# Native sparse attention: GpSimd scales head 1's probabilities, VectorE head 0's; turned tiles and compressed scores laid out anew

## Chip, cores and metric

One core of a Trainium2 chip. The metric is the device time of one execution in microseconds (us); lower is better. The kernel before takes 1884.68 us, the median of 3 runs (1881.19 to 1887.92).

## What is computed

One step of a small decoder trunk: an RWKV-7 layer, a mixture of experts (MoE), shared keys and values, one layer of native sparse attention, a second MoE, and a final norm, all in float32. There are 512 prompt tokens and 32 sample tokens, 16 attention heads of width 64 in 4 key groups, and 16 experts. The part around the change is the attention of the prompt. The selected branch may pick 16 blocks of 64 keys and there are only 8, so the selected and the window branch are both plain causal attention over their own keys; the third branch is over 31 compressed keys:

```python
s_c = einsum('bqgpd,bngd->bqgpn', qg, kc) - slope * d_c
p_c = masked_softmax(s_c, d_c >= 0)             # 31 compressed keys
s_s = einsum('bqgpd,bqgkd->bqgpk', qg, k_s) - slope * d_s
p_s = masked_softmax(s_s, d_s >= 0)
s_w = einsum('bqgpd,bwgd->bqgpw', qg, kw) - slope * d_w
p_w = masked_softmax(s_w, m_w)
o = g[..., 0:1] * (p_c @ v_c) + g[..., 1:2] * (p_s @ v_s) + g[..., 2:3] * (p_w @ v_w)
```

The softmax is divided by its row sum and multiplied by the gate g. In the MoE each token goes through 2 of 16 experts: `combine * ((silu(h @ w_gate) * (h @ w_up)) @ w_down)`.

## The kernel before, in words

Each engine runs a program written out by hand, in order, and engines meet only at semaphores (`wait_ge`, `then_inc`).

**Attention** (`pe_attend` L2948, `act_kv` L3093, `dve_attend` L3269). The 16 heads are taken as 8 pairs j. A unit u is (pair j, query tile i of 128 rows, branch br), 8 units for a pair and 64 in all (NU), then 4 units for the sample. A unit has two heads h of 128*(i+1) keys. For a unit, TensorE makes scores (L2960) into banks 0 to 3; VectorE adds the distances, finds the row minimum and writes to SBUF (L3319); ScalarE takes the exponential in place and the row sums (L3167); VectorE takes the reciprocal of the two sums (L3340), multiplies it by the gates (L3342), and scales both heads' probabilities (L3346, once for each h); TensorE turns them in pieces of 64 rows (L3015) into banks 4 and 5; ScalarE copies these to SBUF (L3157); TensorE multiplies by the values (L3051) into bank 7, which ScalarE stores once for a pair (L3187).

The steps are staggered, and this fixes the order on each engine. At step s VectorE does the scores of unit s and then the weights of unit s-2. ScalarE copies the turned unit s-4 and then does the exponentials of unit s-1. TensorE does, for even s: scores(s), turn(s-4), values(s-6), values(s-5), turn(s-3), scores(s+1). `p_ready` tells TensorE that a unit's probabilities are scaled; four score buffers (NSC) and three turned ones (NPT) limit how far engines run apart.

For the first unit of a pair there is also the compressed branch for all four query tiles: `cmp_scores` (L2981) into bank 6, five VectorE operations of 248 columns (L3327, L3330, L3332, L3352, L3360) with three small ones, two exponentials (L3173), `cmp_turn` (L2990, 8 matmuls against the identity), one copy of 512 columns (L3160), and two matmuls for each query tile with `vcp` (L3047).

GpSimd does nothing in this stage: its queue goes from the MoE of layer 0 (`pool_moe`) to that of layer 1.

**MoE** (`pe_moe` L1960, `act_moe` L2184, `dve_moe` L2323). 16 slots of 96 tokens in each layer, so 32 in all; a slot is one expert's gate, up and down matmuls, with 3 buffers of weights. In a slot TensorE does up, then turns the tokens of a later slot (L2012, 6 transposes of 128x128), waits for VectorE's product silu(gate) times up (L2449), turns that (L2062, 3 transposes), does gate of the next slot, and then down, which waits for the turned product to be copied out by ScalarE (L2236) and VectorE (L2455). The turned tokens are copied out by VectorE (L2440, one operation) and ScalarE (L2220, four).

Of the kernel before, what the change touches and what calls it, by code (L numbers as in the profile page):

```python
# [242 lines left out]
def program(nc, io, out):  # L243
    ctx = ExitStack()
    with ctx:
# [6 lines left out]
        def _(pool):  # L252
# [46 lines left out]
            pool_moe(pool, B, 0, regs)  # L299
            pool_moe(pool, B, 1, regs)  # L300
# [80 lines left out]
        def _(pe):  # L381
# [33 lines left out]
            def key_squares(m):  # L415
                pe.wait_ge(S("ksq_ready"), m + 1)
# [6 lines left out]
            for k in range(KT):  # L423
                pe.wait_ge(S("xm_first"), k + 1)
# [13 lines left out]
            pe.transpose(bank[3][0:72, 0:128], B.lasth[:].rearrange("p n k -> p (n k)"), ident[:]).then_inc(S("last_tr"), 1)  # L438
# [38 lines left out]
        def _(act):  # L477
# [24 lines left out]
            for g in range(2 * KT):  # L502
# [3 lines left out]
                if m >= 0:  # L506
                    if m >= 2:
                        act.wait_ge(S("ksum_mm"), m - 1)
                    act.drain()
                    act.activation((B.hwa, B.hg)[m % 2][:], B.rkv[1][:, m, :], ACT.Square, scale=vec(B, "k_k")[:, m:m + 1]).then_inc(S("ksq_ready"), 1)  # L510
# [20 lines left out]
        def _(dve):  # L531
# [70 lines left out]
            for k in range(KT + 1):  # L602
# [3 lines left out]
                if k:  # L606
                    dve.scalar_tensor_tensor(out=B.xm[0][:, k - 1, :], in0=B.xx[:, k - 1, :], scalar=vec(B, "mix0")[:, k - 1:k],
                                             in1=h[:, k - 1, :], op0=ALU.mult, op1=ALU.add).then_inc(S("xm_first"), 1)
# [13 lines left out]
            dve.wait_ge(S("last_tr"), 1)  # L622
# [1337 lines left out]
def pe_moe(pe, B, l, regs):  # L1960
# [88 lines left out]
    def slot(v, j, left):  # L2049
# [13 lines left out]
        mm.then_inc(S("at_mm"), 1)  # L2063
# [120 lines left out]
def act_moe(act, B, l, regs):  # L2184
# [42 lines left out]
    def slot(v, j, left):  # L2227
# [7 lines left out]
        act.wait_ge(S("at_mm"), s + 1)  # L2235
        act.activation(B.actT[:, 0:2].rearrange("p c t -> p (c t)"), bank[2][:, 0:256], ACT.Copy).then_inc(S("at_ev"), 1)  # L2236
# [86 lines left out]
def dve_moe(dve, B, l, regs):  # L2323
# [1150 lines left out]
```

## Time and profile before

| what | us |
|---|---|
| median of 3 runs | 1884.68 |
| the profiled execution, its own time | 1893.58 |
| its span, first to last instruction | 1891.8 |
| attention stage, 1296 to 1462 of the span | 166 |
| MoE slots of layer 0 and layer 1 | 734 to 1012, 1577 to 1855 |
| TensorE busy in the span | 1767.2 (93%) |
| VectorE, ScalarE, GpSimd busy | 672.5, 512.4, 99.9 |

Times in rows are us from the start of the span; a mean or a duration marked ns is of one instruction. PE is TensorE's matmuls, PEld its weight loads, DVE VectorE, ACT ScalarE, POOL GpSimd. Records of the same kind that follow each other are merged ("x16"). A group has its count, its busy us in sum, the mean ns of one, and the engine's idle us just before. TensorE's matmuls overlap in the records, so its busy time is not a measure of how full it is; the spacing of weight loads is a better one. "[0.63 <-PE bank L2960]" says that the engine stood idle 0.63 us before this instruction and that the matmul of L2960 released it.

### The profile page before, as it was taken

How to read it: one execution, taken by the hardware profiler on the slowest of the kernel's cores; microseconds unless marked ns; L12 is line 12 of the kernel's file. 1: busy time of each engine (PE TensorE's matmuls, PEld its weight loads, DVE VectorE, ACT ScalarE, POOL GpSimd, SP SyncE). 2: the span in 40 equal slices, each digit the busy share in tenths (PEclk: the TensorE clock that was granted, in tenths of full speed). 3: DMA queues.
4: the chain of work that ended last, by engine and by line, in shares of the span. 5: the costliest groups of instructions: out<-in, count | busy, mean ns of one | idle time of the engine just before them, and what ended most of it. 6: DMA issues, size and time to landing. Idle time of an engine off the chain costs nothing.

```text
span 1891.8 us, 53674 instructions
## 1 busy us (share of the span) xinstructions
PE 1767.2 (93%) x23759; PEld 1428.1 (75%) x23759; DVE 672.5 (36%) x1807; ACT 512.4 (27%) x1216; POOL 99.9 (5%) x155
## 2 busy tenths in 40 slices
PE   6999999989998899999999899898989989999997
PEld 4876777777776678999988754687766778999985
DVE  6141226776764332110104300406887240111014
ACT  3112223333332121111113200315887121111113
POOL 2112000000000002000002000000000011000002
PEclk8999999999999999999999999898999997999998
DMA  8666844443434497999978991633000476999944
GB/s 310 212 219 208 266 123 155 135 129 113 118 111 138 139 319 298 376 414 419 417 290 229 244 203 57 196 87 102 2 2 2 124 330 236 411 412 416 417 197 169
DMA packets 195434, 413.68 MB, mean 219 GB/s; under 512 B 53702, under 2 KB 135330, under 8 KB 186722
## 3 DMA queue, kind: packets, MB, share of 16 engines
q1 hardware_dynamic: 176434, 358.08, 55.2%
q0 software_dynamic: 11040, 39.85, 5.8%
q10 hardware_dynamic: 7760, 12.79, 1.9%
q8 instruction: 161, 2.64, 0.6%
q14 instruction: 39, 0.32, 0.1%
HBM read 356.97 MB, written 57.91 MB: 219 GB/s over the span
## 4 chain that ended last, share of the span: by engine, by line
PE 44%; issue 7%; DVE 6%; DMA 2%; DVEq 2%; ACT 1%; POOL 0%; ACTq 0%; SPq 0%
PE bank L2024 12%; PE bank L2019 6%; PE bank L2037 5%; PE bank L2043 4%; PE bank L1746 3%; PE bank L2903 3%; PE bank L2001 2%; PE bank L2012 1%; DVE region_a L3319 1%; DMA region_b<-in_cmp_w_dram 1%; PE bank L2835 1%; DVEq L3341 1%; PE bank L2124 1%; PE bank L3051 1%; PE bank L2062 1%
## 5 line engine op out<-in xcount | busy, mean ns | idle before, releaser
L2019 PE MATMUL bank<-wg,slot_x 128*32 128x384 f32 x1056 | 120.5, 496 | 3.8 <-ACT slot_x L2213 2.4
L2024 PE MATMUL bank<-wg,slot_x 128*32 128x128 f32 x1056 | 121.9, 276 | 0.0
L2019 PE MATMUL bank<-wu,slot_x 128*32 128x384 f32 x1056 | 118.2, 486 | 3.2 <-issue 3.2
L2024 PE MATMUL bank<-wu,slot_x 128*32 128x128 f32 x1056 | 119.1, 273 | 0.0
L2037 PE MATMUL bank<-wd,actT 128*32 128x384 f32 x1056 | 117.7, 486 | 1.3 <-ACT actT L2236 1.3
L2043 PE MATMUL bank<-wd,actT 128*32 128x256 f32 (+1 forms) x704 | 118.3, 326 | 0.0
L2024 PEld LDWEIGHTS bank<-wu,slot_x 128*32 128x32 f32 x1056 | 115.2, 110 | 2.3
L2024 PEld LDWEIGHTS bank<-wg,slot_x 128*32 128x32 f32 x1056 | 115.1, 111 | 0.6
L645 PE MATMUL bank<-xm,wp 128*128 128x272 f32 x480 | 113.5, 395 | 0.0
L645 PEld LDWEIGHTS bank<-xm,wp 128*128 128x128 f32 x480 | 90.2, 190 | 20.8 <-issue 2.7
L2449 DVE TENSOR_TENSOR act<-bank,act 128x384 f32<-128x384 f32 x32 | 17.9, 558 | 245.3 <-PE bank L2024 245.3
L2461 DVE COPY ys<-bank 128x384 f32<-128x384 f32 x32 | 17.9, 558 | 227.4 <-PE bank L2043 227.4
L2043 PEld LDWEIGHTS bank<-wd,actT 128*32 128x32 f32 x704 | 76.7, 110 | 18.4 <-issue 0.4
L2784 PE MATMUL bank<-region_a,fT 128*128 128x512 f32 x192 | 82.7, 593 | 0.0
L2220 ACT ACTIVATE slot_x<-bank,shift_p 128x96 f32<-128x96 f32 x120 | 31.1, 342 | 158.3 <-PE bank L2012 158.3
L2784 PEld LDWEIGHTS bank<-region_a,fT 128*128 128x128 f32 x192 | 36.4, 190 | 45.7 <-issue 45.7
L1178 PE MATMUL bank<-Lp,U 64*64 64x64 f32 x768 | 62.9, 219 | 0.0
L2124 PE MATMUL bank<-region_c,region_b 64*128 64x240 f32 x512 | 55.7, 373 | 7.6 <-DMA region_b<-in_cmp_w_dram 5.5
L1178 PEld LDWEIGHTS bank<-Lp,U 64*64 64x64 f32 x768 | 60.7, 135 | 0.4 <-issue 0.4
L645 PE MATMUL bank<-rkv,wp 128*128 128x272 f32 x256 | 60.2, 394 | 0.0
L2903 PE MATMUL bank<-fT,region_a 128*128 128x272 f32 x256 | 58.9, 393 | 0.0
L2124 PEld LDWEIGHTS bank<-region_c,region_b 64*128 64x128 f32 x512 | 50.2, 191 | 11.6 <-DMA region_b<-in_cmp_w_dram 5.9
(650 smaller groups left out, 3978.5 us busy)
## 6 DMA issues: line engine op xcount, KB each, us to landing
wg<-in_moe_w_gate_dram SPq DMA_DIRECT2D x22, 2048.0 KB, 11.9
wu<-in_moe_w_up_dram SPq DMA_DIRECT2D x22, 2048.0 KB, 16.7
wd<-in_moe_w_down_dram SPq DMA_DIRECT2D x22, 2048.0 KB, 11.8
xT<-in_ada_w_dram SPq DMA_DIRECT2D x40, 1024.0 KB, 5.4
w<-in_moe_w_gate_dram SPq DMA_DIRECT2D x10, 2048.0 KB, 11.9
fT<-in_moe_w_up_dram SPq DMA_DIRECT2D x10, 2048.0 KB, 16.6
gall<-in_moe_w_down_dram SPq DMA_DIRECT2D x10, 2048.0 KB, 11.6
wp<-in_rwkv_w_rkv_dram SPq DMA_DIRECT2D x24, 512.0 KB, 4.2
```

The costliest lines, as they stand in the source:

```text
L645: mm = pe.matmul(B.bank[rkv_bank(n)][:, 0:HALF], B.wp[g % WP][:, k, :], B.xm[g // KT][:, k, half(h)], start=k == 0, stop=k == KT - 1)
L1178: mm = pe.matmul(bank[2][p, i], U[p, h, q], Lp[p, h, q], start=True, stop=True)
L1746: mm = pe.matmul(B.bank[out_bank(q)][:, 0:HALF], w[k], x[:, k, half(h)], start=k == 0, stop=k == KT - 1)
L2001: mm = pe.matmul(bank[6 + h][:, k * C:(k + 1) * C], B.htok[t][0:rows, (4 * h + k) * 128:(4 * h + k + 1) * 128], B.first[t][0:rows], start= ...
L2019: mm = pe.matmul(ps[32 * j:32 * j + 32, 0:GW], x[:, k, 32 * j:32 * j + 32], w[:, k, 0:GW], start=k == 0, stop=k == KT - 1)
L2024: mm = pe.matmul(ps[96:128, q * 128:(q + 1) * 128], x[:, kk, 32 * q:32 * q + 32], w[:, kk, GW:FF], start=kk == 0, stop=kk == KT - 1)
L2037: mm = pe.matmul(bank[4 + b][32 * j:32 * j + 32, 0:384], act_piece(k, j), w[:, k, b * 384:(b + 1) * 384], start=k == 0, stop=k == 3)
L2043: mm = pe.matmul(bank[4 + b2][96:128, at:at + n], act_piece(k, q), w[:, k, col:col + n], start=k == 0, stop=k == 3)
L2124: mm = pe.matmul(o, B.cw1[0][hs(h), l, m * 128:(m + 1) * 128], v, start=l == 0, stop=l == 31)
L2220: ins = act.activation(B.xsT[j][:, k], token_columns(bank[7])[:, q], ACT.Identity, bias=B.shift_p[:, l, k:k + 1])
L2784: mm = pe.matmul(bank[4 + n % 4], B.fT[:, k, cols(t)], B.wkv[:, k, c * 512:(c + 1) * 512], start=k == 0, stop=k == KT - 1)
L2903: mm = pe.matmul(bank[n % 8][:, 0:HALF], B.wq[j % 2][:, k, :], B.fT[:, k, half(h)], start=k == 0, stop=k == KT - 1)
```

## The change

It has three parts. (1) GpSimd scales head 1 of each prompt unit and VectorE head 0; the product with the gates, an operation of its own before, becomes the second scalar of the scaling. TensorE waits for both. (2) The compressed branch: its scores go to free columns of the score banks, with the two heads alternating; the probabilities lie as (tile, head, 32), so that two 128x128 transposes take the place of eight matmuls, and 256 columns are copied in place of 512; `vcp` gets a second copy for odd query tiles, whose rows lie elsewhere. (3) In the MoE both kinds of transposes are cut into halves of 64 rows that go to two banks, so ScalarE and VectorE each copy half of the columns of every tile, and a `sem_inc` instruction stands before them. Some semaphores are renamed and shared.

```diff
@@ gpsimd @@
             pool_moe(pool, B, 0, regs)
+            pool_attend(pool, B)
             pool_moe(pool, B, 1, regs)
+def normalise(eng, B, u, h):
+    j, i, br = UNITS[u]
+    v, g = B.sc[u % NSC][:, h, 0:128 * (i + 1)], 3 * heads(j)[h] + 1 + br
+    return eng.tensor_scalar(v, v, B.sm[u % NSC][:, h:h + 1], B.gates[:, i, g:g + 1], ALU.mult, ALU.mult)
+def pool_attend(pool, B):
+    S = B.sem
+    for u in range(NU):
+        pool.wait_ge(S("dve_rows"), KT + u + 1)
+        normalise(pool, B, u, 1).then_inc(S("side_rows"), 1)
@@ dve_attend, weights @@
-            dve.reciprocal(sm, sm)
+            dve.reciprocal(sm, sm).then_inc(S("dve_rows"), 1)
             dve.drain()
-            dve.tensor_tensor(sm, sm, B.gates[:, i, gate(j, 1 + br)], ALU.mult)
-            dve.drain()
-            for h in range(2):
-                v = B.sc[u % NSC][:, h, 0:nk]
-                ins = dve.tensor_scalar(v, v, sm[:, h:h + 1], None, ALU.mult)
-            ins.then_inc(S("p_ready"), 1)
+            normalise(dve, B, u, 0).then_inc(S("p_ready"), 1)
@@ pe_attend, scores @@
+        if (i, br) == (1, 0):
+            pe.wait_ge(S("scc_read"), j + 1)
...
+        if (i, br) == (0, 0):
+            for i2 in range(4):
+                for h in range(2):
+                    mm = pe.matmul(bank[2 * (u % 2) + h][:, 128 + i2 * NCP:128 + (i2 + 1) * NCP], B.qT[hs(h), j, i2 * 128:(i2 + 1) * 128],
+                                   B.kcT[hs(h), j // HG, NCK:NCK + NCP], start=True, stop=True)
@@ cmp_turn @@
-        for i in range(4):
-            for h in range(2):
-                c = (8 * (j % 2) + 4 * h + i) * NCP
-                mm = pe.matmul(bank[6][hs(h), i * 128:(i + 1) * 128], B.scc_flat[:, c:c + 64], ident[:], start=True, stop=True)
+        for n in range(2):
+            c = 256 * (j % 2) + 128 * n
+            mm = pe.transpose(bank[6][:, n * 128:(n + 1) * 128], B.scc_flat[:, c:c + 128], ident[:])
@@ turn @@
+        pe.wait_ge(S("side_rows"), KT + u + 1)
@@ act_kv @@
-                act.activation(B.PTc[j % 2], bank[6], ACT.Copy).then_inc(S("ptc_ev"), 1)
+                act.activation(B.PTc[j % 2], bank[6][:, 0:256], ACT.Copy).then_inc(S("ptc_ev"), 1)
@@ pe_moe, turn(j, n) @@
+        pe.sem_inc(S("pe_marks"), 1)
         for h in range(2):
             for g in range(QT):
-                mm = pe.transpose(bank[6 + h][:, g * 128:(g + 1) * 128], B.xs[j][:, g, h * 128:(h + 1) * 128], B.ident[:])
-            mm.then_inc(S("x_tr"), 1)
+                for r in range(2):
+                    mm = pe.transpose(turned_rows(bank[6 + r], g)[:, :, :, h], B.xs[j][hs(r), g, h * 128:(h + 1) * 128], B.ident[hs(r), hs(r)])
...
@@ pe_moe, slot @@
         pe.wait_ge(S("act_ready"), s + 1)
+        pe.sem_inc(S("pe_marks"), 1)
         for c in range(3):
-            mm = pe.transpose(bank[2 + c // 2][:, c % 2 * 128:c % 2 * 128 + 128], B.act[:, c, :], B.ident[:])
+            for r in range(2):
+                mm = pe.transpose(bank[2 + r][:, c * 64:c * 64 + 64], B.act[hs(r), c, :], B.ident[hs(r), hs(r)])
@@ act_moe, keep_turned @@
-        for q in range(4):
-            k = 2 * q + 1
-            ins = act.activation(B.xsT[j][:, k], token_columns(bank[7])[:, q], ACT.Identity, bias=B.shift_p[:, l, k:k + 1])
+        for k in range(KT):
+            ins = act.activation(half_tokens(B.xsT[j], 1)[:, k], bank[7][:, 48 * k:48 * k + 48].rearrange("p (g r) -> p g r", g=QT),
+                                 ACT.Identity, bias=B.shift_p[:, l, k:k + 1])
@@ pe_kv, compressed values: each of the 8 prompt matmuls is made twice @@
+                        for e in range(2):
+                            row = 64 * e + r.start // 2
...
@@ dve_kv @@
+    dve.memset(B.vcp[1][:], 0.0)
+    dve.drain()
+    for e in range(2):
+        for h in range(2):
+            rows = slice(64 * e + 32 * h, 64 * e + 32 * h + NCP)
+            ins = dve.tensor_copy(B.vcp[e][rows, :, h, :], bank[6][rows, 256:256 + 2 * HD].rearrange("p (g d) -> p g d", g=2))
```

## Rows read from the trace of the kernel before

**Rows 1.** Windows: length, busy PE, PEld, DVE, ACT, POOL, granted clock, DMA share, GB/s.
```profile
1296.00:1462.00 166.00, 148.74 (x2042) 115.33 (x2041) 140.74 (x624) 136.93 (x446) 0.00 (x0) 0.97 0.05 10
```
**Rows 2.** Timeline of VectorE, where one pair begins and the next (L3319).
```profile
1363.33 0.55 DVE L3319 CUSTOM_DVE_ANT_0 region_a<-tab,bank 128x384 f32<-128x384 f32 x1 [0.63 <-PE bank L2960]
...
1382.03 0.55 DVE L3319 CUSTOM_DVE_ANT_0 region_a<-tab,bank 128x384 f32<-128x384 f32 x1 [0.62 <-PE bank L2960]
```
**Rows 3.** Timeline of VectorE, the weights of one unit of 512 keys.
```profile
1371.72 0.16 DVE L3340 RECIPROCAL region_a<-region_a 128x2 f32<-128x2 f32 x1
1371.95 0.16 DVE L3342 TENSOR_TENSOR region_a<-region_a 128x2 f32<-128x2 f32 x1
1372.19 0.88 DVE L3346 TENSOR_SCALAR region_a<-region_a 128x512 f32<-128x512 f32 x2
1372.99 0.28 DVE L3319 CUSTOM_DVE_ANT_0 region_a<-tab,bank 128x128 f32<-128x128 f32 x1
```
**Rows 4.** Groups by line, VectorE, attention; two forms apart, then all forms together.
```profile
L3346 DVE TENSOR_SCALAR region_a<-region_a 128x128 f32<-128x128 f32 x32 | 7.7, 284 | 1.2
L3346 DVE TENSOR_SCALAR kvtok<-kvtok,region_a 128x512 f32<-128x512 f32 x16 | 7.1, 484 | 1.0 <-issue 0.4
...
L3346 DVE TENSOR_SCALAR region_a<-region_a 128x128 f32<-128x128 f32 (+3 forms) x96 | 31.7, 373 | 3.8
L3346 DVE TENSOR_SCALAR kvtok<-kvtok,region_a 128x256 f32<-128x256 f32 (+1 forms) x32 | 12.0, 417 | 1.9 <-issue 0.9
```
**Rows 5.** Timeline of ScalarE in the same pair: the five places where it waited.
```profile
1369.19 0.88 ACT L3157 ACTIVATE region_a<-bank 128x384 f32<-128x384 f32 x2 [0.92 <-PE bank L3015]
...
1373.93 1.09 ACT L3157 ACTIVATE region_a<-bank 128x512 f32<-128x512 f32 x2 [0.55 <-PE bank L3015]
...
1376.26 1.08 ACT L3157 ACTIVATE region_a<-bank 128x512 f32<-128x512 f32 x2 [0.48 <-PE bank L3015]
...
1379.09 0.60 ACT L3160 ACTIVATE region_a<-bank 128x512 f32<-128x512 f32 x1 [0.44 <-PE bank L2990]
...
1381.05 0.60 ACT L3187 ACTIVATE fT<-bank 128x512 f32<-128x512 f32 x1 [0.39 <-PE bank L3051]
```
**Rows 6.** Groups by line, ScalarE: a copy of 256 columns.
```profile
L3157 ACT ACTIVATE region_a<-bank 128x256 f32<-128x256 f32 x20 | 6.6, 383 | 0.0
```
**Rows 7.** Timeline of TensorE's weight loads in the same pair.
```profile
1373.12 0.58 PEld L3015 LDWEIGHTS bank<-ident,region_a 64*128 64x128 f32 x16 [1.90 <-DVE region_a L3346]
...
1377.94 0.85 PEld L2990 LDWEIGHTS bank<-ident,region_a 128*64 128x64 f32 x16 [0.26 <-DVE region_a L3360]
```
**Rows 8.** GpSimd: two groups by line, and a timeline with what released it.
```profile
L1859 POOL TENSOR_TENSOR actT<-actT,rstd 128x256 f32<-128x256 f32 x2 | 1.4, 725 | 569.4 <-ACT rstd L715 569.4
L289 POOL MEMSET seg_start<- 128x544 f32 x1 | 0.6, 556 | 0.1
...
617.96 0.75 DVE L1447 TENSOR_REDUCE ssq<-ysq 128x9 f32<-128x576 f32 x1
618.80 0.20 POOL L1430 TENSOR_SCALAR rstdy<-ssq 128x9 f32<-128x9 f32 x1 [28.43 <-DVE ssq L1447]
```
**Rows 9.** Timeline of one MoE slot, from up to the next gate and down.
```profile
831.72 0.64 PEld L2012 LDWEIGHTS bank<-ident,slot_x 128*128 128x128 f32 x6 [0.20 <-issue]
...
831.83 0.56 DVE L2449 TENSOR_TENSOR act<-bank,act 128x384 f32<-128x384 f32 x1 [7.14 <-PE bank L2024]
...
832.44 0.31 PEld L2062 LDWEIGHTS bank<-ident,act 128*128 128x128 f32 x3
...
832.64 1.03 ACT L2220 ACTIVATE slot_x<-bank,shift_p 128x96 f32<-128x96 f32 x4 [5.47 <-PE bank L2012]
832.92 0.12 PEld L2019 LDWEIGHTS bank<-wg,slot_x 128*32 128x32 f32 x3 [0.17 <-issue]
...
838.10 0.11 PEld L2043 LDWEIGHTS bank<-gall,actT 128*32 128x32 f32 x1
```
**Rows 10.** One line of the trace: TensorE's own semaphore instruction.
```profile
L3045 PEldq EVENT_SEMAPHORE  x7: 51/51/51, 1325.7 to 1438.6; - x7
```

More of the change, by code:

```diff
@@ L2643, in allocate_nsa @@
     B.gtmp = view(A, at + 776, 2, 48)
-    B.scc = [view(A, at + 872 + 248 * i, 2, 4, NCP) for i in range(2)]
-    B.scc_flat = view(A, at + 872, 2 * 248 + 64 - NCP)
+    B.scc = [view(A, at + 872 + 256 * i, 4, 2, 32) for i in range(2)]
+    B.scc_flat = view(A, at + 872, 512)
     B.sc = [view(A, i * 1024, 2, 512) for i in range(3)] + [B.kvtok[:, 2:4, 0:512]]
-    B.PTc = [view(A, 3072 + i * 512, 512) for i in range(2)]
+    B.PTc = [view(A, 3072 + i * 256, 256) for i in range(2)]
     B.osb = B.kvtok[:, 0, 0:512]
@@ L2858, in compressed @@
                         mm = pe.matmul(o, B.cw2[:, z, m, :], B.hid[z][:, m, at:at + w], start=m == 0, stop=m == 1)
-                    else:
-                        o = bank[6][0:w, g * HD:(g + 1) * HD] if part == 0 else bank[6][r.start:r.start + w, 256 + gp * HD:256 + (gp + 1) * HD]
-                        mm = pe.matmul(o, B.hid[z][:, m, at:at + w], B.cw2[:, z, m, :], start=m == 0, stop=m == 1)
+                    elif part == 0:
+                        mm = pe.matmul(bank[6][0:w, g * HD:(g + 1) * HD], B.hid[z][:, m, at:at + w], B.cw2[:, z, m, :], start=m == 0, stop=m == 1)
+                    else:
+                        for e in range(2):
+                            row = 64 * e + r.start // 2
+                            mm = pe.matmul(bank[6][row:row + w, 256 + gp * HD:256 + (gp + 1) * HD], B.hid[z][:, m, at:at + w], B.cw2[:, z, m, :],
+                                           start=m == 0, stop=m == 1)
         mm.then_inc(S("cmp_mm"), 1)
@@ L2973, in sample_scores @@
           .then_inc(S("sc_mm"), 1)
-    def cmp_scores(j, h):
-        if h:
-            pe.wait_ge(S("scc_mm"), 2 * j + 1)
-        elif j >= 1:
-            pe.wait_ge(S("ptc_ev"), j)
-        for i in range(4):
-            mm = pe.matmul(bank[6][:, (4 * h + i) * NCP:(4 * h + i + 1) * NCP], B.qT[hs(h), j, i * 128:(i + 1) * 128],
-                           B.kcT[hs(h), j // HG, NCK:NCK + NCP], start=True, stop=True)
-        mm.then_inc(S("scc_mm"), 1)
     def cmp_turn(j):
         pe.wait_ge(S("pc_ready"), j + 1)
-        for i in range(4):
-            for h in range(2):
-                c = (8 * (j % 2) + 4 * h + i) * NCP
-                mm = pe.matmul(bank[6][hs(h), i * 128:(i + 1) * 128], B.scc_flat[:, c:c + 64], ident[:], start=True, stop=True)
+        if j >= 1:
+            pe.wait_ge(S("ptc_ev"), j)
+        for n in range(2):
+            c = 256 * (j % 2) + 128 * n
+            mm = pe.transpose(bank[6][:, n * 128:(n + 1) * 128], B.scc_flat[:, c:c + 128], ident[:])
         mm.then_inc(S("ptc_tr"), 1)
@@ L3046, in values @@
             for h in range(2):
-                pe.matmul(o[h], B.vcp[:, j // HG, h, :], B.PTc[j % 2][:, i * 128:(i + 1) * 128], start=True, stop=False)
+                pe.matmul(o[h], B.vcp[i % 2][:, j // HG, h, :], B.PTc[j % 2][:, i // 2 * 128:(i // 2 + 1) * 128], start=True, stop=False)
         for kt in range(i + 1):
@@ L3056, in step_scores @@
             return
-        first = u < NU and UNITS[u][1:] == (0, 0)
-        if first:
-            cmp_scores(UNITS[u][0], 0)
         scores(u)
-        if first:
-            cmp_scores(UNITS[u][0], 1)
     def step_turn(u):
@@ L3193, in dve_kv @@
     dve.memset(B.kvTp[:].rearrange("p z l (g n) -> p (z l g) n", g=2)[:, :, NCP:32], 0.0)
-    dve.memset(B.vcp[:], 0.0)
+    dve.memset(B.vcp[0][:], 0.0)
     dve.tensor_tensor(B.pair[:], B.ident[:, 0:64], B.ident[:, 64:128], ALU.add)
@@ L3355, in dve_attend @@
                 dve.drain()
-                dve.tensor_tensor(B.smc, B.smc, table(B, "row_valid").unsqueeze(1).to_broadcast([128, 2, 4]), ALU.mult)
+                dve.tensor_tensor(B.smc, B.smc, table(B, "row_valid").unsqueeze(2).to_broadcast([128, 4, 2]), ALU.mult)
                 dve.drain()
-                dve.tensor_tensor(B.smc, B.smc, B.gates[:, 0:4, gate(j, 0)].rearrange("p i h -> p h i"), ALU.mult)
+                dve.tensor_tensor(B.smc, B.smc, B.gates[:, 0:4, gate(j, 0)], ALU.mult)
                 dve.drain()
```

63 lines of the change are left out of this document (33 added, 30 removed).

## The prediction

> **What bounds the kernel now.** I first looked for the stage that the change is about and read the busy times of the engines in it, then one pair of heads in VectorE's timeline, then the same pair in ScalarE's and TensorE's, and last the MoE slot and GpSimd's rows.
>
> The attention stage is 166 us long, TensorE, VectorE and ScalarE are each busy for 137 to 149 of it, GpSimd for nothing, and DMA moves next to nothing [rows 1]. So whatever is saved here moves everything after it forward by the same amount. The stage is a repetition of 8 pairs. A pair takes 1382.03 - 1363.33 = 18.70 us, and VectorE waits in it once for TensorE, 0.62 us [rows 2]; the other small gaps are those between dependent operations of its own. VectorE therefore needs 18.70 - 0.62 = 18.08 us for a pair. ScalarE waits five times in the same pair, 0.92 + 0.55 + 0.48 + 0.44 + 0.39 = 2.78 us, and so needs 15.92 [rows 5]. TensorE's largest wait in the pair, 1.90 us, is for VectorE's scaling [rows 7]. The reader is to see that VectorE sets the pace, and that ScalarE follows 2.2 us behind it: that is the room.
>
> **Part 1, the scaling.** In a unit, VectorE now does reciprocal, gates, scaling twice [rows 3]. The product with the gates goes: from its start to the next start, 1372.19 - 1371.95 = 0.24 us, 8 times in a pair, 1.92 us. The second scaling goes: the mean of one over all sizes is (96 x 373 + 32 x 417) / 128 = 384 ns [rows 4], and neighbours overlap by 0.08 (a pair of 0.484 takes 1372.99 - 1372.19 = 0.80 to the next start [rows 3, 4]), so 0.30 x 8 = 2.40 us. VectorE's need falls from 18.08 to 13.76 us for a pair. No row shows a scaling with two scalars in memory. From below it costs the same; from above it would lose its speed of (484 - 284) / 384 = 0.52 ns an element [rows 4] and take twice that, 320 keys on average x 0.52 = 0.17 us more a unit, 1.3 a pair: 15.1, still under ScalarE. I take no extra cost.
>
> GpSimd gets 64 scalings of 320 elements on average. Its fixed share is about 0.20 us (9 elements take that), its nearest rows are a memset, 556 / 544 = 1.02 ns an element with everything in it, and a product of two tensors, 725 / 256 = 2.83 ns [rows 8]. So 0.33 to 0.91 us for a mean unit. A scaling reads one tensor, not two, which puts it nearer the memset: I take 0.50. A unit lasts 18.70 / 8 = 2.34 us, so GpSimd is not the bound at either end. GpSimd's queue is otherwise empty here, so nothing stands behind it. Who waits for it is TensorE's turn, two or three steps after. Before, both heads are scaled 1373.07 - 1371.88 = 1.19 us after the reciprocal's end in a unit of 512 keys; after, GpSimd starts about 0.09 us after VectorE's end [rows 8] and needs 0.52 to 1.45 for 512, so it is ready after 0.6 to 1.5 us, or 0.5 later if it must let VectorE's scaling by first. About as late as before: this wait can take back a part, not all.
>
> **Part 2, the compressed branch.** `cmp_turn` loads 16 times in 0.85 us [rows 7]; two 128x128 transposes are 2 x 0.64 / 6 = 0.21 us [rows 9]. The work is directly before a copy for which ScalarE waited 0.44 us [rows 5]; I count that wait as gone. The copy of 512 columns took 0.60 us [rows 5], one of 256 takes 0.38 [rows 6]: ScalarE's need falls by 0.22 to 15.70 us a pair. The compressed scores are as many matmuls as before, with the heads alternating; they lie where TensorE waits for VectorE, and I count nothing (from 0 to 0.5 us a pair for the better). The wait for `scc_read` holds TensorE's scores two units later until one more VectorE operation is done; a whole step lies between, so nothing, at worst 0.4 a pair. The doubled matmuls for the compressed values: 16 more records with 64 columns of weights or so, 0 to 0.85 us by the 16 loads [rows 7]; I take 0.5, once. VectorE's additional memset and copies there lie under the query projections; without that cover they would be some 1 us.
>
> **Part 3, the MoE, 32 slots.** The turn of the tokens (six loads, 0.64 us) ends at 832.36. VectorE's product ends at 831.83 + 0.56 = 832.39, and its own transposes start at 832.44 [rows 9]. So a shorter token turn only makes TensorE wait longer for VectorE: the first `sem_inc` and the first halves are covered by the product, by some 0.3 us. The second part is on the path: three loads in 0.31 us become six of 64 rows, which take 0.58 / 16 = 0.036 us each in attention [rows 7], 0.22 us, and the second `sem_inc` adds 0.05 [rows 10]. That is -0.04 us a slot, -1.3 in all. From above: no faster loads and both marks on the path, +0.10 x 32 = +3.2; from below -0.09 x 32 = -2.9. ScalarE makes 8 copies of 48 in place of 4 of 96, which take 1.03 us [rows 9]: I estimate 0.6 us more from these. In the loop the copies begin at 832.64 and down needs ScalarE's next result at 838.10 [rows 9], so this is covered by 4 us and more; only in the first slot of each layer TensorE waits for them, 2 x 0.6 = +1.2. Part 3 is thus 0 us, between -3 and +4.4.
>
> **The sum.** After the change ScalarE is the slowest with 15.70 us a pair. Of its waits I keep the 0.39 us before L3187 (the last values of a pair, data that are late for their own reasons) and a quarter of the three before L3157, 1.95 x 0.25 = 0.5 us, because the turn now follows GpSimd too. That makes 16.6 us a pair, 2.1 less than 18.70, and 8 x 2.1 = -16.8 us. With +0.5 and 0: -16.3 us. The profiled execution took 1893.6 us, so it would be 1877.3; the median of the runs shown is 1884.7, 8.9 less, and I put the same difference on it: 1868.4, say 1868 us.
>
> **Rivals.** *The port.* VectorE starts its scaling 0.07 us after the reciprocal's end (1371.95 against 1371.88 [rows 3]), GpSimd 0.09 after its releaser [rows 8]: near a tie on nearly the same memory, and if GpSimd holds a path that VectorE's scaling needs, VectorE stands for up to its whole operation. Price: 8 x 0.33 to 0.91 us, so VectorE needs 16.4 to 21.0 us a pair. It decides from (18.70 - 13.76) / 8 = 0.62 us of GpSimd time a unit; at 0.91 it is +2.3 x 8 = +18.6, 1904 us, slower. At my 0.50 it is 17.8 us a pair, or -7, 1878 us. For it: the tie. Against it: VectorE is 0.02 us ahead, and behind the scaling come operations that read one tensor in memory and one in PSUM. No row of this trace has both engines at it.
> The Trainium skill, SBUF — State Buffer, "Who interferes with whom", says that this pair of ports is an exclusive lock for a VectorE operation that uses both of its ports and for any of GpSimd, held for the whole instruction by whoever is first. The skill's GPSIMD Engine Reference, "Engine selection", says that GpSimd is about twice as slow with two inputs and near line rate with one; by that rule the price stays at its low end and this rival does not reach the point where it decides.
>
> *TensorE is the real bound.* Three of ScalarE's waits are for TensorE's turns [rows 5]. If those come from TensorE's own work and not from VectorE, only the shorter `cmp_turn` counts: 0.64 x 8 = -5, with +0.5 some -4.6, 1880 us. Against it: TensorE's 1.90 us of waiting [rows 7].
>
> *All of ScalarE's waits vanish.* 15.70 us a pair, -24 us, with part 3 at its best -26: 1859 us. Against it: orders written out by hand seldom fit so well.
>
> **Chances.** The forecast, with its own range of 1861 to 1876: 0.60. All waits gone: 0.11. The port with a GpSimd of middling speed, 1876 to 1879: 0.11. TensorE the bound, or part 3 at its worst beside a weak part 1, within 0.3% (5.7 us, about what a measurement of this kernel can tell from no change): 0.11. The port with a slow GpSimd: 0.07. So faster 0.82, same 0.11, slower 0.07, and 8 in 10 lie in 1859 to 1882.
>
> **What would show it.** Right: from pair to pair 16.3 to 17 us in VectorE's timeline; VectorE with waits of its own for TensorE or ScalarE; L3167 and L3157 without gaps; GpSimd's scalings of 512 at 0.5 to 0.8 us; slots of the MoE as long as before within 0.1 us. Wrong: VectorE's scaling of 512 longer than 0.48 us or starting later than 0.07 after the reciprocal (the port, or a slower form); TensorE's turn released by GpSimd in most units; more than 0.3 us between the product in the MoE and the next gate than now.

## The result and the profile after

The changed kernel takes 1871.89 us (median of 6 runs, 1864.13 to 1877.48), the kernel before, beside it, 1885.88 us (6 runs): ratio 0.9922, 95% interval 0.9901 to 0.9944, 14 us less. The profiled execution took 1871.2 us (span 1869.4), that of before 1893.6 (span 1891.8); the 22 us between these two overstate the change: 8.2 us of them are already there where the attention stage begins (VectorE's first operation on scores is at 1296.99 and at 1288.77), and 16.9 us arise in the stage, which takes 159.43 us before and 142.50 us now from its first to its last such operation.

Page of the changed kernel, busy time of each engine:
```profile
PE 1737.4 (93%) x23939; PEld 1400.7 (75%) x23939; DVE 652.4 (35%) x1682; ACT 525.8 (28%) x1336; POOL 149.3 (8%) x219
```
GpSimd has 64 instructions and 49 us more than before, VectorE 125 instructions and 20 us less.

Windows of the changed kernel, two pairs of heads, cut at the start of ScalarE's copy of a finished pair (columns as in [rows 1]):
```profile
1312.15:1328.91 16.76, 15.18 (x228) 11.69 (x230) 13.40 (x56) 15.51 (x52) 6.08 (x8) 1.00 0.01 3
1328.91:1345.51 16.60, 15.16 (x230) 11.74 (x232) 13.31 (x56) 15.52 (x53) 6.08 (x8) 1.00 0.01 2
```
Four of its six pairs take 16.59 to 16.77 us, the others 16.83 and 16.93. Cut at the same place, the kernel before gives 18.69 and 19.05 us for its pairs. Over the six pairs that lie between the first and the seventh of these copies the mean was 18.81 us, and is now 16.72 us. This mean is the measure for all kernels below, called "the pair"; where a pair without a fallen clock or another disturbance is meant, the text says "undisturbed".

Timeline of VectorE, the pair's beginning, its 512 unit and the next beginning (answers to [rows 2] and [rows 3]):
```profile
1313.12 0.56 DVE L3347 CUSTOM_DVE_ANT_0 region_a<-tab,bank 128x384 f32<-128x384 f32 x1 [1.73 <-PE bank L2979]
...
1320.31 0.16 DVE L3368 RECIPROCAL region_a<-region_a 128x2 f32<-128x2 f32 x1
1320.57 0.55 DVE L3199 TENSOR_SCALAR region_a<-region_a 128x512 f32<-128x512 f32 x1
...
1322.55 0.42 DVE L3347 CUSTOM_DVE_ANT_0 region_a<-tab,bank 128x256 f32<-128x256 f32 x1 [0.31 <-PE bank L3031]
...
1329.89 0.56 DVE L3347 CUSTOM_DVE_ANT_0 region_a<-tab,bank 128x384 f32<-128x384 f32 x1 [1.73 <-PE bank L2979]
```
VectorE now waits 1.73 + 0.31 us in 16.77, so it needs 14.73 us. (This is the first of the two pairs above, cut at VectorE's operation.)

GpSimd in the same pair, its scaling of a 256 unit and of the first 512 unit, and TensorE's turn behind the latter:
```profile
1314.34 0.67 POOL L3199 TENSOR_SCALAR kvtok<-kvtok,region_a 128x256 f32<-128x256 f32 x1 [2.68 <-DVE region_a L3368]
...
1320.57 1.02 POOL L3199 TENSOR_SCALAR region_a<-region_a 128x512 f32<-128x512 f32 x1 [1.54 <-DVE region_a L3368]
```
```profile
1321.69 0.71 PE L3031 MATMUL bank<-ident,region_a 64*128 64x64 f32 x16 [1.26 <-POOL region_a L3199]
```
The two engines begin at the same 1320.57; TensorE's turn is released by GpSimd, 0.5 us after VectorE is done.

The chain of waits through this pair, shortened:
```profile
1313.12 0.56 DVE region_a L3347
...
1320.57 1.03 POOL region_a L3199
...
1321.69 0.71 PE bank L3031 x16
...
1324.81 1.09 ACT region_a L3168 x2
...
1329.14 0.73 PE bank L2979 x4
...
1329.89 0.56 DVE region_a L3347
```
So this pair is a loop: VectorE from 1313.12 to 1320.57, GpSimd's scaling of the 512 unit, then TensorE, with ScalarE's copies of one unit in it, to 1329.87. No engine is busy all the way round. The next two pairs, of 16.59 us each by the same cut, have a detour at their start in place of VectorE's own work, to GpSimd's scaling of a 256 unit and TensorE's turn and scores behind it, before VectorE goes on:
```profile
1329.89 0.56 DVE region_a L3347
...
1331.11 0.68 POOL kvtok L3199
...
1331.88 0.46 PE bank L3031 x8
1332.34 0.93 PE bank L2979 x4
...
1333.30 0.68 DVE kvtok L3347
...
1337.16 1.03 POOL region_a L3199
...
1342.97 0.37 PE bank L3005 x2
```
GpSimd's scaling is thus a link at two units of the eight, and the last line is TensorE's compressed turn, also a link.

The MoE slot at 827, answering to [rows 9]:
```profile
827.11 0.45 PEld L2015 LDWEIGHTS bank<-ident,slot_x 64*128 64x128 f32 x12 [0.20 <-issue]
...
827.22 0.56 DVE L2461 TENSOR_TENSOR act<-bank,act 128x384 f32<-128x384 f32 x1 [7.14 <-PE bank L2028]
...
827.76 1.64 ACT L2226 ACTIVATE slot_x<-bank,shift_p 128x48 f32<-128x48 f32 x8 [5.20 <-PE bank L2015]
827.89 0.29 PEld L2068 LDWEIGHTS bank<-ident,act 64*128 64x128 f32 x6 [0.33 <-issue]
...
828.26 0.12 PEld L2023 LDWEIGHTS bank<-wg,slot_x 128*32 128x32 f32 x3
```
From the product's end to the next gate it is 0.48 us where it was 0.53. From product to product, a slot takes 16.96 us instead of 17.01, in nearly all intervals of the two layers. But the slot behind each layer's loop is another matter. The windows below are of layer 1, product to product: the slot behind the loop after the change, and then, in the kernel before, the one slot of layer 1 that is longer than its neighbours, which is the next one (in that kernel the slot behind the loop itself takes 17.02 us, with a DMA share of 1.02):
```profile
1767.33:1791.95 24.62, 20.16 (x292) 17.02 (x294) 2.02 (x4) 2.85 (x11) 0.00 (x0) 0.86 0.90 367
```
```profile
1813.88:1831.16 17.28, 17.24 (x281) 15.13 (x281) 1.87 (x5) 2.29 (x7) 0.00 (x0) 1.00 0.36 133
```
In it, the timeline of TensorE shows a stop that nothing in the profile explains, and matmuls at half speed behind it (three 384-column products per 0.64 us instead of 0.32):
```profile
1783.76 0.80 PE L2023 MATMUL bank<-wu,slot_x 128*32 128x384 f32 x1 [4.23 <-issue]
...
1784.84 1.00 PE L2023 MATMUL bank<-wu,slot_x 128*32 128x384 f32 x3
```
In layer 0 the slot behind the loop took 18.48 us, before 20.91. Together 43.10 against 38.19 us (20.91 + 17.28): +4.9.

### The profile page after: what moved, and what is told of

Its sections match the earlier page's. It is cut to its first block, busy times and chain, and to the rows that moved or that the text cites. A ratio compares the mean times of both kernels' runs of the same rounds, so it can differ in the third digit from the quotient of the medians.

```text
span 1869.4 us, 54094 instructions
## 1 busy us (share of the span) xinstructions
PE 1737.4 (93%) x23939; PEld 1400.7 (75%) x23939; DVE 652.4 (35%) x1682; ACT 525.8 (28%) x1336; POOL 149.3 (8%) x219
## 4 chain that ended last, share of the span: by engine, by line
PE 45%; issue 8%; DVE 5%; ACT 2%; DMA 2%; POOL 1%; DVEq 1%; ACTq 0%; SPq 0%
PE bank L2028 12%; PE bank L2023 6%; PE bank L2041 5%; PE bank L2047 4%; PE bank L1747 3%; PE bank L2920 3%; PE bank L2002 1%; PE bank L3067 1%; PE bank L3031 1%; DMA region_b<-in_cmp_w_dram 1%; DVE act L2461 1%; PE bank L2848 1%; PE bank L2131 1%; DVE region_a L3347 1%; PE bank L2068 1%
## 5 line engine op out<-in xcount | busy, mean ns | idle before, releaser
L2226 ACT ACTIVATE slot_x<-bank,shift_p 128x48 f32<-128x48 f32 x240 | 49.3, 316 | 155.9 <-PE bank L2015 155.9
L3199 POOL TENSOR_SCALAR region_a<-region_a 128x128 f32<-128x128 f32 (+3 forms) x48 | 35.1, 730 | 330.6 <-DVE region_a L3368 330.6
L654 ACT ACTIVATE rkv<-bank 128x272 f32<-128x272 f32 x48 | 19.0, 397 | 146.6 <-PE bank L646 137.9
## 6 DMA issues: line engine op xcount, KB each, us to landing
fT<-in_moe_w_up_dram SPq DMA_DIRECT2D x10, 2048.0 KB, 16.9
```

Of the source, the lines that this page charges most:

```text
L2226: ins = act.activation(half_tokens(B.xsT[j], 1)[:, k], bank[7][:, 48 * k:48 * k + 48].rearrange("p (g r) -> p g r", g=QT), ACT.Identity, b ...
```

## The experiments

For each kernel: the pair, and "the stalls", the sum of the lengthened slot of each layer (the one behind the loop; in the kernel before and in part 1 alone, layer 1's is the next one), both from its profiled execution. A minus or plus in us against before is the ratio times 1885.

**Which part brings what.** Part 1 alone on the kernel before (the attention's scaling and its semaphores):
```diff
-            dve.tensor_tensor(sm, sm, B.gates[:, i, gate(j, 1 + br)], ALU.mult)
...
-            for h in range(2):
...
+            normalise(dve, B, u, 0).then_inc(S("p_ready"), 1)
```


> The kernel before with only the split of the scaling (GpSimd head 1, VectorE head 0, both in the two-scalar form); compressed branch and MoE as before. Theory (VectorE's occupancy set the pair): nearly all of the gain is here. VectorE loses 8 gate products (0.24 us) and 8 scalings (0.39 us) per pair and pays 8 x 0.06 us for the other form, 4.5 us; the pair falls from 18.70 us to about 17.1 us, since TensorE keeps its slow compressed scores and turn (about 1 us per pair more than after the whole change), and the program takes about 1873 us, ratio about 0.994. Rival (the parts act only together, since the half of the pair that TensorE owns must shrink as well): pair about 18 us, ratio 0.997 to 0.998. Rival (the gain of the whole change is elsewhere): ratio 1.000.

Measured: ratio 0.9946 (0.9927 to 0.9964), pair 17.63 us, stalls 38.4. Faster, but the pair is 0.5 us longer than the occupancy theory has it, and VectorE waits in it:
```profile
DVE region_a L3335 <- PE bank L2961: 2.2, 1, 2.2
...
DVE region_a L3335 <- PE bank L3017: 0.8, 2, 0.5
```
(Waits in one pair: total, times, longest.) With 3.0 us of waits VectorE does not set this pair. Its chain has the same loop, with TensorE's compressed scores (L2982) and its compressed turn of 16 matmuls (L2991) in it:
```profile
1343.28 0.56 DVE region_a L3335
...
1347.73 0.49 PE bank L2982 x5
...
1351.09 1.03 POOL region_a L3190
...
1356.91 1.02 PE bank L2991 x16
```
From VectorE's first operation to the 512 scaling it is 1351.09 - 1343.28 = 7.81 us, against 1337.16 - 1329.89 = 7.27 in the changed kernel, and the compressed turn with the four matmuls behind it takes 1.24 us against 0.74. These 0.54 + 0.50 us are the 1.03 us between 17.63 and 16.60.

The changed kernel without part 1, that is, parts 2 and 3:

> The changed kernel without the split: VectorE forms the gated reciprocals and scales both heads as before; compressed branch and MoE as changed. Theory (VectorE's occupancy set the pair): VectorE's need of 18.1 us per pair is back, the pair is 18.2 to 18.6 us, ratio to before 0.997 to 1.000 (1880 to 1885 us). Rival (TensorE's compressed scores and turn were a bound of their own): pair about 17.6 us and ratio 0.994 to 0.996 even without GpSimd.

Measured: ratio 1.0022 (0.9998 to 1.0046), stalls 42.9 us. Its pairs come in two kinds, here one of each:
```profile
1317.42:1335.62 18.20, 15.65 (x228) 11.70 (x230) 15.62 (x69) 15.68 (x52) 0.00 (x0) 1.00 0.01 2
1335.62:1355.24 19.62, 17.18 (x230) 13.15 (x231) 17.27 (x75) 15.68 (x53) 0.00 (x0) 0.91 0.01 2
```
The undisturbed pair is 0.49 us shorter than before, as the theory of this run has it; the ratio, expected at 0.997 to 1.000, is not. In three of six pairs the granted clock falls, and they are 1.4 us longer: mean 18.90. The fall comes behind TensorE's wait of 1.47 us for VectorE's scaling of the 512 unit; in the 4 us after it the clock is at its lower level, 1.2 GHz, for most of the time (0.58 on the mean):
```profile
1346.41 0.71 PE L3029 MATMUL bank<-ident,region_a 64*128 64x64 f32 x16 [1.47 <-DVE region_a L3372]
...
1347.53 1.50 PE L3065 MATMUL bank<-kvtok 128*64 128x128 f32 x12
```
```profile
1346.41:1350.50 4.09, 4.09 (x48) 3.69 (x50) 3.57 (x19) 1.84 (x6) 0.00 (x0) 0.58 0.00 0
```
Twelve of these products take 1.50 us here; in the kernel before they took 0.83:
```profile
1373.13 0.71 PE L3015 MATMUL bank<-ident,region_a 64*128 64x64 f32 x16 [1.50 <-DVE region_a L3346]
...
1374.04 0.83 PE L3051 MATMUL bank<-region_a,kvtok 128*64 128x128 f32 x12
```
The kernel before has the same wait, 1.50 us, and keeps its clock in all six pairs, with 16.64 us of TensorE's busy time in a pair against 15.65 here. That this shorter work around an unchanged wait lost the clock is a reading of these rows and not shown: the three undisturbed pairs of this kernel have the same wait of 1.47 us in the same program, and keep theirs.

The changed kernel without part 3 (the MoE stage as before):

> The changed kernel with the MoE stage as before: only the attention stage is changed. Theory: the MoE halves are worth 0.05 us per slot, some 1.4 us over the two layers, and the memset and extra small products of the key and value stage cost 0.5 us; so this kernel takes 1872 to 1874 us, ratio 0.993 to 0.994, the same as the whole change within 1.5 us. Rival (the MoE part is a cost or a gain that the stall after the loop hid): this kernel is 3 us or more away from the changed one, either way.

Measured: ratio 0.9923 (0.9895 to 0.9951), as the whole change; pair 16.65 us, slots 17.02, stalls 42.5 us. By the ratio it is within 1.5 us of the changed kernel, as expected, though the intervals of some 4 to 5 us cannot tell 1.5 us. Its stalls are nearly those of the changed kernel (22.56 + 19.94 us) although its MoE code is that of before: what sets them is not the MoE edit alone.

Both heads on VectorE, each in the two-scalar form, GpSimd idle, the rest as changed:
```diff
-            normalise(dve, B, u, 0).then_inc(S("p_ready"), 1)
+            normalise(dve, B, u, 0)
+            normalise(dve, B, u, 1).then_inc(S("p_ready"), 1)
```


> The changed kernel with both heads' scalings on VectorE in the two-scalar form, GpSimd idle in the stage. Tells what the 62 ns are that VectorE's scaling took longer after the change (347, 412, 479, 546 ns at 128, 256, 384, 512 columns against 284, 351, 418, 484 before). If they are the form's own cost: the same 347 to 546 ns here, VectorE's need is 14.7 + 8 x 0.45 = 18.3 us per pair, the pair 18.5 to 18.8 us, time 1883 to 1888 us. If they are the shared use of memory beside GpSimd: 284 to 484 ns here, need 14.2 + 8 x 0.39 = 17.3 us, pair 17.6 to 18 us, time 1877 to 1881 us.

Measured: ratio 0.9970 (0.9946 to 0.9994); four of six pairs 17.55 to 17.58 us, two with a fallen clock (0.90 and 0.91) 18.99 and 19.14, mean 18.06. Groups of the attention stage, by form:
```profile
L3197 DVE TENSOR_SCALAR region_a<-region_a 128x128 f32<-128x128 f32 x28 | 8.5, 345 | 1.1
L3197 DVE TENSOR_SCALAR kvtok<-kvtok,region_a 128x512 f32<-128x512 f32 x14 | 7.0, 543 | 0.6
```
284 and 484 ns in [rows 4], 345 and 543 here with GpSimd idle: the 0.06 us belong to the form, not to GpSimd. The slope stays at 0.52 ns an element. The expected pair for this case, 18.5 to 18.8, was too long (and the time, 1882.15 us, is just under the expected 1883 to 1888) by what two neighbouring scalings overlap: 14.73 + 2.9 (a second scaling adds 0.26, 0.33, 0.39 and 0.46 us to the first at 128 to 512 columns, twice each) = 17.6, which is the pair. Here VectorE is the bound (0.4 us of waits), and its second scaling is what GpSimd takes off it.

**What GpSimd's time is made of.** First, GpSimd waits for VectorE's scaling instead of the reciprocals:
```diff
-        pool.wait_ge(S("dve_rows"), KT + u + 1)
+        pool.wait_ge(S("p_ready"), u + 1)
```


> The changed kernel, but GpSimd begins its scaling when VectorE has ended its own (it waits for p_ready instead of the reciprocals). Tells whether GpSimd's 1.36 ns per column is its own speed or contains time in which VectorE's scaling beside it holds it up. Own speed: 499, 672, 846 and 1020 ns at 128 to 512 columns stay; the turn of the 512 unit comes 0.46 us later and the pair goes from 16.6 us to 17.0 to 17.3 us. Held up: GpSimd takes 0.84 ns per column or so (the slope between its two MEMSETs is at most that), 0.75 us at 512 columns, and the pair stays within 0.3 us of 16.6 us.

Second, GpSimd waits as in the changed kernel, and VectorE waits for it before its own scaling:
```diff
+            dve.wait_ge(S("side_rows"), KT + u + 1)
             normalise(dve, B, u, 0).then_inc(S("p_ready"), 1)
```


> The changed kernel, but VectorE waits before its own scaling until GpSimd's is done, so that GpSimd runs with VectorE idle. Own speed of GpSimd: 499 to 1020 ns as in the changed kernel. Held up by VectorE's scaling: 0.40 to 0.75 us. VectorE stands still for GpSimd's 0.76 us on average plus 0.1 us for the signal, 8 times a pair: need 14.7 + 6.9 = 21.6 us per pair and about 1912 us in the one case; 19 to 20 us per pair in the other.

Measured, groups of GpSimd in the attention stage: the changed kernel (two), and behind VectorE (two). Before VectorE the means are the same 447 and 767 ns.
```profile
L3199 POOL TENSOR_SCALAR region_a<-region_a 128x512 f32<-128x512 f32 x8 | 8.2, 1019 | 13.1 <-DVE region_a L3368 13.1
L3199 POOL TENSOR_SCALAR region_a<-region_a 128x128 f32<-128x128 f32 x14 | 7.0, 500 | 21.7 <-DVE region_a L3368 21.7
```
```profile
L3199 POOL TENSOR_SCALAR region_a<-region_a 128x128 f32<-128x128 f32 x14 | 6.3, 447 | 26.6 <-DVE region_a L3199 26.6
...
L3199 POOL TENSOR_SCALAR region_a<-region_a 128x512 f32<-128x512 f32 x7 | 5.4, 767 | 12.9 <-DVE region_a L3199 12.9
```
Apart from VectorE's scaling, GpSimd takes 447, 554, 661 and 767 ns for 128 to 512 columns, on either side of it; beside it 500, 673, 846 and 1019. The slope alone is (767 - 447) / 384 = 0.83 ns a column, beside it (1019 - 500) / 384 = 1.35, and the difference, 0.52, is VectorE's own time per element. So GpSimd stands for as long as VectorE's scaling moves data. It does not stand beside VectorE's operation on the scores: in the kernel where it comes second it has that one beside it and takes 0.77 us. The first kernel's pair is outside both of its expectations: five of six take 17.37 or 17.38 us, one, with the granted clock at 0.91, 19.31, mean 17.70. GpSimd's own time came out as the second case had it, but the pair did not stay within 0.3 us of 16.6. The 17.37 us fit the loop, by a sum made after the run: GpSimd ends 0.51 - 0.12 = 0.39 us later at the 256 unit and 0.65 - 0.25 = 0.40 us later at the 512 unit (VectorE's start to GpSimd's, less what it is shorter), together 0.79; 16.60 + 0.79 = 17.39. Those are the two units at which GpSimd is a link in the chain of the 16.60 us pair. Time 1880.28 us in one run. The second kernel's pair is 20.4 us (1897.83 us in one run), between the two cases, with the clock at 0.92 in it.

Then VectorE's scaling begins a little later, behind two small memsets with drains, or one without:
```diff
+            dve.memset(B.gtmp[:], 0.0)
             normalise(dve, B, u, 0).then_inc(S("p_ready"), 1)
```


> The changed kernel with two small memsets (96 columns) on VectorE between the reciprocals and its scaling, so that GpSimd is already in its scaling when VectorE's begins. If the two engines shut each other out of memory, VectorE's scaling, now second, gets longer or later: 0.55 us at 512 columns becomes 0.9 us or more. If they don't, VectorE keeps 347 to 546 ns and GpSimd 499 to 1020 ns, and only the memsets (about 0.15 us each with their drain) lengthen VectorE's side, 2 to 2.5 us per pair, of which its 2.0 us of waits hide a part: pair 17.0 to 18.5 us.

> The changed kernel with one memset of 96 columns (0.14 us) between VectorE's reciprocals and its scaling, so that VectorE's scaling begins some 0.15 us after GpSimd's and lies beside it nearly whole. Lock that belongs to the first: VectorE's scaling of 512 columns is drawn out from 0.55 us to 0.8 us or more and GpSimd keeps the 0.77 us it takes alone. VectorE always goes first: VectorE keeps 0.55 us and GpSimd takes 1.0 us. Both slowed a little: something between. Pair 16.7 to 17.5 us.

Measured, one 512 unit with two memsets, GpSimd and VectorE:
```profile
1362.76 0.77 POOL L3199 TENSOR_SCALAR region_a<-region_a 128x512 f32<-128x512 f32 x1 [2.25 <-DVE region_a L3368]
```
```profile
1363.29 0.55 DVE L3199 TENSOR_SCALAR region_a<-region_a 128x512 f32<-128x512 f32 x1
```
Begun 0.53 us after GpSimd, neither is longer than alone, though they lie side by side for 0.24 us. With one memset the scaling begins 0.10 us after GpSimd:
```profile
1356.50 1.05 POOL L3199 TENSOR_SCALAR region_a<-region_a 128x512 f32<-128x512 f32 x1 [1.54 <-DVE region_a L3368]
```
```profile
1356.60 0.47 DVE L3199 TENSOR_SCALAR region_a<-region_a 128x512 f32<-128x512 f32 x1
```
VectorE is not held (0.47), and GpSimd, although its record begins first, takes 1.05. Which of the two was first at the memory no record tells: 0.34 us of GpSimd's time alone (447 ns less 128 x 0.83) does not grow with the columns, so it may move no data yet when VectorE begins 0.10 us later. No group of VectorE's 512-column scalings in these runs has a mean more than 0.02 us above the 546 ns of the changed kernel. Pairs: 18.5 to 20.2 us with two memsets (1888.09 us in one run; 19.2 on the mean, above the expected range), 16.73 with one (1874.14 us in one run). That VectorE can be made to wait, with the two starting still otherwise, is not excluded: a start between 0.10 and 0.53 us after GpSimd's was not tried.

**Is it the loop?** In the changed kernel the three operations on the compressed scores (1.33 us) stand ahead of the 512 unit's scaling. Here they follow it:
```diff
-            if (i, br) == (0, 0):
-                C = B.scc[j % 2][:].rearrange("p i h n -> p (i h) n")[:, :, 0:NCP]
...
             normalise(dve, B, u, 0).then_inc(S("p_ready"), 1)
+        if s < NU and UNITS[s][1:] == (0, 0):
+            j = UNITS[s][0]
...
```


> The changed kernel with one thing moved: where a pair of heads begins, VectorE scales the 512 unit first and only then does its three operations on the compressed scores (1.33 us from 1318.99 to 1320.31 in the changed kernel's timeline), which now stand ahead of that scaling. Theory (the pair is a loop: VectorE's part from 1313.12 to 1320.57, GpSimd's 512 scaling 1.03 us, TensorE's part from 1321.69 to 1329.87): the loop loses up to 1.2 us, until ScalarE's 15.5 us per pair holds it; pair 15.6 to 16.0 us, 8 pairs give 5 to 8 us, time 1863 to 1867 us, ratio to before 0.988 to 0.990. Rival (ScalarE's or TensorE's occupancy already sets 16.6 us): pair 16.4 us or more, ratio 0.992 as the changed kernel. Rival (the compressed exponentials come later and hold ScalarE up): pair over 16.6 us.

Measured: ratio 0.9909 (0.9879 to 0.9940), median 1868.53, pair 16.29 us. The loop does give way, by 0.43 us (0.35 between undisturbed pairs, 16.60 and 16.25), but only by a third of the 1.2 us, and the pair lies between the expected 16.0 and the rival's 16.4. The times themselves do not tell it from the changed kernel (0.9922, 0.9901 to 0.9944). VectorE's path to the 512 scaling is out of the chain, and another is as long, through ScalarE's copies and exponentials:
```profile
1335.17 0.87 ACT kvtok L3168 x2
1336.04 0.88 ACT kvtok L3178 x3
...
1337.44 0.77 ACT region_a L3168 x2
...
1338.35 0.71 PE bank L3031 x16
```
Besides this, the copy of a finished pair moved from ScalarE to VectorE:
```diff
-        if s % 8 == 5 and s > 8:
-            act_store_heads(act, B, s // 8 - 1)
...
+        dve.tensor_copy(B.fT[:, j, 0:SEQ], bank[7]).then_inc(S("o_ev"), 1)
```


> The kernel with the compressed operations after the scaling, and besides the copy of a finished pair of heads (128x512 out of PSUM, 0.60 us, once per pair) moved from ScalarE to VectorE, where it falls into the 1.61 us that VectorE waits for TensorE's 384 scores. Theory: with 16.25 us per pair, ScalarE is left with 0.39 + 0.46 us of waits, so it holds the pair; without the copy its need falls from 15.4 us to 14.9 us, the pair to 15.6 to 15.9 us, 3 to 5 us in eight pairs, time 1862 to 1866 us. Rival (TensorE's own part of the loop or VectorE, now with 15.3 us of need, holds it): pair 16.1 us or more, time unchanged at 1867 to 1869 us.

Measured: ratio 0.9898 (0.9866 to 0.9930), median 1866.26, pair 16.24 us: the rival. ScalarE's busy time fell from 15.40 to 14.92 and the pair did not follow. From 1341.94 to 1348.70 the chain consists of ScalarE's copies and exponentials alone, and then goes on with TensorE; neither VectorE nor GpSimd is in it. In the kernel without this edit the moved copy was a link in one of two pairs that I followed, with ScalarE's copies of a 256 unit 1347.70 - 1345.58 = 2.12 us behind its start. Here they are again 1341.94 - 1339.82 = 2.12 us behind it, now released by TensorE's turn after a wait of 0.17 us: TensorE's path to this point was as long as ScalarE's.

And TensorE waits for GpSimd only ahead of head 1's transposes:
```diff
-        pe.wait_ge(S("side_rows"), KT + u + 1)
...
         for h in range(2):
+            if h:
+                pe.wait_ge(S("side_rows"), KT + u + 1)
```


> As the kernel with the head copy on VectorE, and TensorE waits for GpSimd's rows only ahead of head 1's transposes, not ahead of head 0's, which VectorE has scaled 0.26 to 0.47 us sooner. Theory (GpSimd's scaling is a link of the loop wherever its end is later than VectorE's and TensorE waits there): 0.2 to 0.35 us for each of one or two units per pair, pair 15.3 to 15.7 us, time 1859 to 1864 us, 1 to 4 us below the kernel without it. Rival (ScalarE or TensorE holds the pair): no difference of more than 1 us.

Measured: ratio 0.9918 (0.9888 to 0.9948), pair 16.21 us: the rival again. GpSimd's scaling had left the chain already in the kernel that this edit was made on, so the edit had nothing to gain there. It was not tried on the changed kernel, where GpSimd is a link at two units.

**The stall behind the loop.** 32 empty instructions on TensorE ahead of layer 1's MoE stage, on the kernel with the head copy on VectorE:

> The kernel with the head copy on VectorE, and 32 empty instructions on TensorE ahead of the MoE stage of layer 1, where it waits for other engines anyway. They change nothing but where the code behind them lies. In all kernels with the MoE halves the slot behind layer 1's loop takes 24.4 to 24.6 us instead of 16.96 us (TensorE stands 4.2 us for nothing that the profile shows, then runs at half clock), in the kernel before 17.3 us. If the stall is a matter of where the code lies when the loop is left (code that has to be brought in while the weights of a slot fill the DMA engines), that slot changes by over 1 us, at best to 17 us: time 1859 to 1861 us; it may as well get worse. If it belongs to the MoE edit itself (its order or its waits), the slot stays at 24.4 to 24.6 us and the time within 1 us of the kernel without the empty instructions, or up to 2 us more.

Measured: ratio 0.9916 (0.9889 to 0.9943), the slot behind layer 1's loop 24.39 us. A shift by 32 instructions does not move the stall; other shifts were not tried. What sets it stays open: in all eleven kernels with the MoE halves the slot behind the loop in layer 1 takes 24.25 to 24.63 us; in the three with the old form layer 1's lengthened slot takes 17.28, 17.48 (both one slot later) and 19.94.

**Does it add up?** Eight pairs at their mean against 18.81, the stalls against 38.2, and 26 slots x 0.05 = 1.3 us where the MoE is changed:

| kernel | pairs | stalls, slots | sum | by the ratio | the stage itself |
|---|---|---|---|---|---|
| part 1 alone | -9.4 | +0.2 | -9.2 | -10.2 | -8.3 |
| parts 2 and 3 | +0.7 | +4.7 - 1.3 | +4.1 | +4.1 | +0.4 |
| parts 1 and 2 | -17.3 | +4.3 | -13.0 | -14.5 | -17.1 |
| the change | -16.7 | +4.9 - 1.3 | -13.1 | -14.7 | -16.9 |
| compressed operations later | -20.2 | +4.7 - 1.3 | -16.8 | -17.2 | -18.2 |

The last column is what the stage really lost in the profiled execution, from VectorE's first operation on scores to its last. It bears out eight times the pair but for the last kernel, where that is 2.0 us too much. The ratios are uncertain by 3.5 to 6 us, so this supports the accounting and does not prove the stalls' share, which comes from profiled executions alone.

## Why the prediction was right, and where its steps were not

The time: 1868 us forecast, 1871.9 measured, in the range of 1859 to 1882, and in the forecast's own range of 1861 to 1876. The saving was forecast as 16.3 us and is 14.0 between the medians, 14.7 by the ratio. The pair: 18.70 less 2.1 was forecast, and it is 16.60 where undisturbed, 16.72 on the mean.

- **VectorE's need.** Forecast 13.76 us, found 14.73. The gates' product and the second scaling went as said; of the difference of 0.97, 0.5 is the form (0.06 us, 8 times), which I had bounded by 0.17 and taken as nothing, and 0.2 is the step from the start of the reciprocals to the next start, 0.26 us now and 0.23 before, 8 times. The rest I did not follow.
- **GpSimd.** 0.50 us taken for a mean unit, 0.76 found, inside the bounds of 0.33 to 0.91. Of it 0.61 is its own and 0.15 waiting for VectorE. At 512 columns 1.02 us, not 0.5 to 0.8.
- **Who sets the pair.** This step was wrong, though its number held. I let ScalarE set it with 15.70 us and 0.9 us of kept waits. It needs 15.52 and waits 1.25, but the chain touches it for one unit's copies; the pair is the loop of VectorE, GpSimd and TensorE. The chain shows this, the 17.37 us with GpSimd behind VectorE fit it, and the reordering tested it: with three of VectorE's operations taken out of the loop the pair is 0.35 to 0.43 us shorter. Moving ScalarE's copy is no test of the changed kernel, since it was done where ScalarE was already in the chain. That 15.70 and 0.9 add up to the pair that was found is luck: the first is 0.2 us too much, the second 0.35 too little, and neither is what the pair waits for.
- **The parts.** I gave part 1 nearly the whole. Alone it brings 1.18 us a pair, part 2 alone (its undisturbed pairs) 0.49, both together 2.16 (the kernel without part 3). Each shortens another stretch of one loop: with VectorE's stretch shortened first, part 2 (the step from 17.63 to 16.60) brings 1.03 us and not 0.49.
- **Compressed turn and copy.** Forecast 0.21 and 0.38 us; the timeline has 0.20 for the two loads and 0.39 for the copy. The compressed scores, counted as nothing, are now 16 matmuls in one piece of 1.01 us.
- **MoE.** -0.04 us a slot forecast, -0.05 found; ScalarE's copies 0.6 us longer as estimated (1.64 against 1.03), and hidden. The +1.2 us for the first slots did not come: the first interval is 18.83 and 18.82 us, before 18.79 and 18.75. The slots behind the loops, +4.9 us, stood nowhere in the prediction; with the -1.3 us of the slots that is +3.6 us in the profiled executions, about what the forecast was short of (3.9 us), though the runs cannot tell so little apart with certainty. The half microsecond of the key and value stage was not isolated.
- **The port rival.** Something of the kind exists, the other way round: GpSimd gives way to VectorE, also where its record begins 0.10 us earlier, and VectorE never stood. VectorE's scaling of 512 was indeed longer than 0.48 us, which I had put down as a sign of this rival or of a slower form: it was the form. The Trainium skill, SBUF — State Buffer, "Who interferes with whom", describes a lock held by whoever is first for its whole instruction. The exclusion itself the runs bear out, at 0.52 ns a column. If the one whose record begins first were the first, VectorE would have waited in the run with one memset, for 0.8 us or more at 512 columns, and it took 0.47; but which engine was first at the memory the records do not show, so that part stays open.
- **TensorE as the real bound.** Half true: with VectorE relieved alone, TensorE's compressed scores and turn are what keeps the pair at 17.63 and not at 16.60.

## What to carry to other kernels

When engines hand a piece of work round a loop, none is saturated and the pace is the sum of the links: read the chain of waits over one period, and shorten or move out what lies in it (the three operations moved behind the scaling took no work away and shortened the pair by 0.43 us). Look for the next path too: that move brought a third of what was taken out, and 0.48 us less of ScalarE's work brought nothing, because TensorE's path was as long. Price an offload with both engines at work on the memory, not from rows of one alone. And look at the granted clock in each period: with parts 2 and 3 alone, three of six pairs lost 1.4 us by it, more than the 0.49 us that the edit saves.

## What was not expected of the hardware

- A scaling by two per-partition scalars in memory takes VectorE 0.06 us longer than one by a single scalar, at every length from 128 to 512 columns, and keeps its 0.52 ns an element.
- GpSimd's record of a scaling contains the time in which VectorE's scaling holds it up: 1.02 us beside it, 0.77 us apart from it, at 512 columns; it begins where VectorE's begins, and grows by 0.52 ns a column. Nothing in the record calls it a wait.
- TensorE stands still for 4.9 us in its weight loads (4.2 in its matmuls, both "issue") in the slot behind layer 1's loop, where the slot's DMA share is 0.90, and then runs at half speed, 1.2 GHz, for some 5 us (granted clock 0.86 over the slot). The slot cost 7.3 to 7.7 us more than its neighbours in layer 1 of every kernel with the changed MoE stage; in the kernel before it cost nothing, at a DMA share of 1.02, and the next one 0.3 us. In layer 0 it is the other way: 3.9 us more than its neighbours before, 1.5 us after. Why is open.
